# The first modulation weight taken in four channel slices in the front stage of a hybrid decoder layer

## The reference, cut to what matters

```python
mod = jax.nn.silu(c) @ w_ada[l] + b_ada[l]          # 1024 -> 6 x 1024
sh1, sc1, g1, sh2, sc2, g2 = [m[:, None, :] for m in jnp.split(mod, 6, axis=-1)]
u = x * (1.0 + sc1) + sh1
proj = u @ w_in                                     # ... | q | k | v | ...
```

## Time and profile before

| | |
|---|---|
| median of 3 runs | 2750.84 us (2745.45 to 2751.7) |
| profiled execution, its own time | 2748.32 us |
| span of its profile | 2746.4 us |
| PE busy | 2492.0 us, 91% |
| DVE busy | 1461.8 us, 53% |
| ACT busy | 1116.5 us, 41% |
| POOL busy | 831.0 us, 30% |
| DMA | 549.61 MB, mean 200 GB/s |

### The profile page before, as it was taken

The page is one execution under the profiler, slowest core; times in us unless marked ns, Lnnn a source line. Parts: engine busy times, 40 slices in busy tenths (PEclk is TensorE's granted clock), DMA queues, the critical chain, the costliest instruction groups (busy, mean ns, idle before and its releaser), DMA issues. The chain is left out here.

```text
span 2746.4 us, 36119 instructions
## 1 busy us (share of the span) xinstructions
PE 2492.0 (91%) x12521; PEld 2082.2 (76%) x12522; DVE 1461.8 (53%) x1898; ACT 1116.5 (41%) x1818; POOL 831.0 (30%) x707
## 2 busy tenths in 40 slices
PE   5999899999999999999989979995998999999960
PEld 4788678778888888888868858874887888887850
DVE  6222156665665656566653256774447445526636
ACT  3122144554454545454531022213547545526633
POOL 2111022442222222222212226575222222223236
PEclk9999899999999999999999989996999999999985
DMA  7699676767665666676446746433558646627736
GB/s 262 248 311 321 240 219 187 250 199 231 194 214 176 213 210 198 193 244 196 150 157 207 208 154 238 161 108 136 162 153 290 181 142 203 192 61 227 253 70 245
DMA packets 258781, 549.61 MB, mean 200 GB/s; under 512 B 23860, under 2 KB 93608, under 8 KB 258024
## 3 DMA queue, kind: packets, MB, share of 16 engines
q1 hardware_dynamic: 236072, 483.07, 53.0%
q0 software_dynamic: 15248, 46.62, 7.6%
q10 hardware_dynamic: 7344, 18.35, 1.7%
HBM read 394.94 MB, written 153.02 MB: 200 GB/s over the span
## 5 line engine op out<-in xcount | busy, mean ns | idle before, releaser
L93 PE MATMUL mx_acc<-u_u,mx_w_hi 128*128 128x512 f32 x1792 | 569.8, 399 | 4.0 <-DMA mx_w_lo<-halves 4.0
L722 POOL TENSOR_TENSOR mx_wt<-mx_wt,mx_rest 128x127 f32<-128x127 f32 (+15 forms) x128 | 271.5, 2121 | 743.4 <-DVE mx_rest L924 743.4
L93 PEld LDWEIGHTS mx_acc<-u_u,mx_w_hi 128*128 128x128 f32 x1792 | 325.5, 189 | 68.4 <-DMA mx_w_lo<-halves 4.8
L932 DVE TENSOR_TENSOR mx_wt_lo<-mx_p_t,mx_wt_hi 128x512 fp32r<-128x512 f32 (+2 forms) x320 | 192.2, 605 | 326.9 <-ACT mx_wt_hi L887 325.1
L93 PE MATMUL mx_acc<-u_u,mx_w_lo 128*128 128x512 f32 x896 | 352.0, 393 | 0.0
L887 ACT ACTIVATE mx_wt_hi<-mx_p_t 128x512 fp32r<-128x512 f32 (+2 forms) x320 | 170.9, 534 | 408.6 <-PE mx_p_t L774 361.5
L924 DVE TENSOR_TENSOR_SCAN mx_rest<-mx_rest,mx_zero 128x128 f32<-128x128 f32 (+15 forms) x128 | 314.2, 2455 | 8.8 <-ACT mx_wt L869 8.8
L93 PE MATMUL moe_p_gu<-keep_wide_hi,moe_x_hi 128*128 128x512 f32 x656 | 262.6, 400 | 14.1 <-DVE keep_wide_lo L1936 13.0
L93 PE MATMUL moe_p_gu<-keep_wide_hi,moe_x_lo 128*128 128x512 f32 x656 | 258.1, 393 | 0.0
L93 PE MATMUL moe_p_gu<-keep_wide_lo,moe_x_hi 128*128 128x512 f32 x656 | 257.8, 393 | 0.0
L868 ACT ACTIVATE mx_rest<-mx_p_z 128x512 f32<-128x512 f32 (+2 forms) x320 | 171.1, 535 | 100.1 <-PE mx_p_z L761 59.2
(11 more groups left out here) (250 smaller groups left out, 5134.1 us busy)
## 6 DMA issues: line engine op xcount, KB each, us to landing
mx_w_hi<-halves SPq DMA_DIRECT2D x98, 512.0 KB, 3.7
mx_w_lo<-halves SPq DMA_DIRECT2D x98, 512.0 KB, 5.3
keep_stay<-in_w_gate SPq DMA_DIRECT2D x64, 512.0 KB, 5.2
keep_stay<-in_w_up SPq DMA_DIRECT2D x64, 512.0 KB, 6.1
keep_stay<-in_w_down SPq DMA_DIRECT2D x32, 1024.0 KB, 6.9
u_saved<-u_u SPq DMA_DIRECT2D x4, 4096.0 KB, 19.5
mx_w_mod<-in_w_ada SPq DMA_DIRECT2D x64, 256.0 KB, 5.1
gate_t<-mx_g_out SPq DMA_DIRECT2D x64, 256.0 KB, 5.0
```

The costliest lines, as they stand in the source:

```text
L93: mm = pe.matmul(out, a, b, start=first and n == 0, stop=last and n == len(pairs) - 1, skip_group_check=True)
L722: pool.tensor_tensor(wt[:, t % 2, 0:w - 1], wt[:, t % 2, 0:w - 1], rest[:, t % 2, 1:w], ALU.mult).then_inc(m["weights_done"], 1)
L932: dve.tensor_tensor(wt_lo[:, first:first + k - j], p_t[:, n % TR, 0:(k - j) * P].rearrange("p (j t) -> p j t", t=P), f32(wt_hi[:, first:fi ...
```

## The change

The first 2048 columns of `w_ada` are loaded and summed in four slices of 256 shift and 256 scale channels, that is two groups `k` each. A slice is eight DMAs of 256 KB in pieces of 1 KB, into `ada`, a double buffer in `stay`, which nothing else uses in this stage. Slices 1 to 3 are put in SP's queue ahead of weight pieces 2, 4 and 6; slice i waits for the sums of slice i - 2. DVE sums slice i + 1, and adds it to `mod` after PE's column sums, ahead of the weight rests of the two groups of slice i; each of its eight steps waits for the one before. PE's column sums of slices 2 and 3 stand behind parts 1 and 3, in a bank of their own, so that TR is 3. A transpose for part k + 3 now stands behind part k.

For block 0 ACT makes the high part of u itself. The rests of the second column half go from DVE to GpSimd, behind u's eighth rest. ACT takes second-half pieces 8 to 11 ahead of the evictions, 12 and 13 behind that of unit 1, and 14 and 15 behind that of unit 3. SP's weight loads 12 to 15 wait for GpSimd's rests 1 to 4, and `load_x(1)` and `save(0)` still come behind them.

```diff
-    AB, TR = 4, 4
+    AB, TR = 4, 3
...
+        ada = flat(stay, 1).rearrange("p (b k h n) -> p b k h n", b=2, k=KD, h=2)
...
             # gpsimd
+                if n == KD - 1:
+                    for j in range(KD):
+                        pool.wait_ge(m["w_hi_done"], KD + j + 1)
+                        pool.tensor_tensor(w_lo[:, j, WH:2 * WH], ring[:, j % RS, 0:WH], f32(w_hi[:, j, WH:2 * WH]), ALU.subtract
+                                           ).then_inc(m["w2_lo_done"], 1)
...
             # sync
+            def load_slice(i):
+                past(sp, m["summed"], KD * (i - 1))
+                for q in range(SLICES):
+                    for h in range(2):
+                        sp.dma_start(ada[:, i % 2, SK * q:SK * (q + 1), h], ada_view[:, SK * q:SK * (q + 1), h * D + i * SC:h * D + (i + 1) * SC]
+                                     ).then_inc(ada_in[i % 2][q], 16)
+
+            def load_w(n):
+                half, k = divmod(n, KD)
+                if n < KD + RS:
+                    past(sp, m["w_lo_done"], n - RS + 1)
+                else:
+                    sp.wait_ge(m["w2_lo_done"], n - RS - KD + 1)
...
+            load_slice(0)
             sp.dma_start(xr[:], x_view[:, 0]).then_inc(m["x_in"], 16)
             for n in range(2 * KD):
+                if n < KD and n > 0 and n % SK == 0:
+                    load_slice(n // SK)
+                load_w(n)
...
             # tensor
+            sum_rows(0)
             for k in range(TR):
                 turn(0, k)
+            sum_rows(1)
             pe.wait_ge(m["cols_out"], 2)
             for k in range(KD):
+                pe.wait_ge(m["u_lo_done"], k + 1)
+                pe.wait_ge(m["w_lo_done"], k + 1)
+                for i in range(AB):
+                    part(0, i, k)
                 if TR + k < KD:
                     turn(0, TR + k)
+                if (k + 1) % SK == 0 and k // SK + 2 < SLICES:
+                    sum_rows(k // SK + 2)
             for tb in range(TB):
                 for i in range(AB if tb == 0 else 0, UNITS):
                     if tb == 0 and i == WH // P:
-                        pe.wait_ge(m["w_lo_done"], 2 * KD)
+                        pe.wait_ge(m["w2_lo_done"], KD)
...
             # scalar
             for k in range(KD):
+                act.wait_ge(m["mod_step"], k // SK + 2)
                 affine(0, k)
+                act.wait_ge(m["affine"], k + 1)
+                act.activation(u[:, 0, 0, k], uf[:, k % 2], ACT.Copy).then_inc(m["u_hi_done"], 1)
                 high_w(k)
-            for n in range(KD, 2 * KD):
+            for n in range(KD, KD + RS):
                 high_w(n)
...
+                if n in (1, 3):
+                    for j in range(2):
+                        high_w(KD + RS + n - 1 + j)
...
             # vector
+            def sum_slice(i):
+                for k in range(KD):
+                    dve.wait_ge(ada_in[i % 2][k // SK], 32 * (i // 2 + 1))
+                    if k == 0:
+                        ins = dve.tensor_scalar(msum[:, i], ada[:, i % 2, 0], csilu[:, 0:1], None, ALU.mult)
+                    else:
+                        dve.wait_ge(m["summed"], KD * i + k)
+                        ins = dve.scalar_tensor_tensor(out=msum[:, i], in0=ada[:, i % 2, k], scalar=csilu[:, k:k + 1],
+                                                       in1=msum[:, i], op0=ALU.mult, op1=ALU.add)
+                    ins.then_inc(m["summed"], 1)
+                dve.wait_ge(m["mod_summed"], i + 1)
+                dve.wait_ge(m["mod_step"], i + 1)
+                cols, sums = (v.rearrange("p (h k) -> p h k", h=2)[:, :, SK * i:SK * (i + 1)]
+                              for v in (mod[:, 0:FIRST_COLS], p_mod[:, 0:FIRST_COLS]))
+                dve.tensor_tensor(cols, cols, sums, ALU.add).then_inc(m["mod_step"], 1)
...
-            for k in range(KD):
-                high(0, k)
-                low_w(k)
-            for n in range(KD, 2 * KD):
-                low_w(n)
+            sum_slice(0)
+            for i in range(SLICES):
+                if i + 1 < SLICES:
+                    sum_slice(i + 1)
+                for k in range(SK * i, SK * (i + 1)):
+                    low_w(k)
```

More of the change, by code:

```diff
@@ L137, in load_piece, with front @@
             bass.ds(e, 1), :, a - KD:b - KD].rearrange("e p k d -> p (e k) d")).then_inc(piece_in[i], 16)
-def front(nc, used, keep, x, c, w_ada, b_ada, w_conv, w_in, u, u_in, u_saved, qk_hi, qk_lo, v_tok, halves):
+def front(nc, used, keep, stay, x, c, w_ada, b_ada, w_conv, w_in, u, u_in, u_saved, qk_hi, qk_lo, v_tok, halves):
     ident, mod, conv_cols, csilu, one = (keep[n] for n in ("ident", "mod", "conv_cols", "csilu", "one"))
     VR = NJ + KD + 3 * KC
-    MW = FIRST_MOD * NB
     QW, QKW = 3 * AW, 2 * AW
@@ L148, in front @@
     UNITS = QKT + NB // P
-    AB, TR = 4, 4
+    AB, TR = 4, 3
     RS = 4
-    MH, WH = MW // 2, QW // 2
+    WH = QW // 2
+    SLICES = 4
+    SC = D // SLICES
+    SK = KD // SLICES
     c_q = 3 * CH
@@ L155, in front @@
         vec = s.sb("vec", [VR, P])
-        ring = s.sb("ring", [P, RS, MH])
+        ring = s.sb("ring", [P, RS, D])
+        ada = flat(stay, 1).rearrange("p (b k h n) -> p b k h n", b=2, k=KD, h=2)
         xr = s.sb("x", [P, NB // P, D])
@@ L160, in front @@
         stage = s.sb("stage", [P, 2, 2 * NB])
-        acc, p_t = s.ps("acc", [P, AB, NB]), s.ps("p_t", [P, TR, NB])
-        p_vec, p_mod = acc[:, AB - 1, 0:VR], acc[:, AB - 2, 0:FIRST_COLS]
+        acc, p_t, p_mod = s.ps("acc", [P, AB, NB]), s.ps("p_t", [P, TR, NB]), s.ps("p_mod", [P, NB])
+        p_vec = acc[:, AB - 1, 0:VR]
         names = ("vec_in", "vec_turned", "ident_step", "silu_done", "cols_out", "summed", "mod_summed", "mod_step",
-                 "x_in", "turned", "affine", "u_hi_done", "u_lo_done", "w_hi_done", "w_lo_done", "pe_done", "act_out",
+                 "x_in", "turned", "affine", "u_hi_done", "u_lo_done", "w_hi_done", "w_lo_done", "w2_lo_done", "pe_done", "act_out",
                  "dve_out", "fill_hi_done", "fill_lo_done")
@@ L169, in front @@
         ring_in = [s.sem(f"ring_in{i}") for i in range(RS)]
+        ada_in = [[s.sem(f"ada_in{b}{i}") for i in range(SLICES)] for b in range(2)]
         block = ctx.enter_context(nc.Block())
-        msum = stage
+        msum = stage[:].rearrange("p a b -> p (a b)").rearrange("p (s h n) -> p s h n", s=SLICES, h=2)
         x_view = x.rearrange("b (g t p) d -> (b p) g t d", p=P, t=NB // P)
@@ L193, in _ @@
             sp.dma_start(vec[NJ + KD:VR, :], w_conv.rearrange("l t (r p) -> (l t r) p", p=P)).then_inc(m["vec_in"], 16)
[L194 to L198, removed]
+            def load_slice(i):
[10 more added lines that the diff above has]
+                    sp.wait_ge(m["w2_lo_done"], n - RS - KD + 1)
+                sp.dma_start(ring[:, n % RS, 0:WH], in_view[:, k, c_q + half * WH:c_q + (half + 1) * WH]
+                             ).then_inc(ring_in[n % RS], 16)
+            load_slice(0)
             sp.dma_start(xr[:], x_view[:, 0]).then_inc(m["x_in"], 16)
             for n in range(2 * KD):
[L201 to L207, removed]
+                if n < KD and n > 0 and n % SK == 0:
+                    load_slice(n // SK)
+                load_w(n)
             def load_x(tb):
@@ L219, in load_fill @@
                 if n == 0:
-                    sp.wait_ge(m["w_lo_done"], 2 * KD)
+                    sp.wait_ge(m["w2_lo_done"], KD)
                 col = fill_column(n)
@@ L294, in part, with sum_rows @@
                     mm.then_inc(m["pe_done"], 1)
[L296 to L302, removed]
+            def sum_rows(i):
+                pe.wait_ge(m["summed"], KD * (i + 1))
+                for h in range(2):
+                    for j in range(SK):
+                        n = h * KD + i * SK + j
+                        mm = pe.matmul(p_mod[:, n:n + 1], msum[:, i, h, j * P:(j + 1) * P], one[:], start=True, stop=True,
+                                       skip_group_check=True)
+                mm.then_inc(m["mod_summed"], 1)
+            sum_rows(0)
             for k in range(TR):
                 turn(0, k)
+            sum_rows(1)
             pe.wait_ge(m["cols_out"], 2)
             for k in range(KD):
+                pe.wait_ge(m["u_lo_done"], k + 1)
+                pe.wait_ge(m["w_lo_done"], k + 1)
+                for i in range(AB):
+                    part(0, i, k)
                 if TR + k < KD:
                     turn(0, TR + k)
[L309 to L314, removed]
+                if (k + 1) % SK == 0 and k // SK + 2 < SLICES:
+                    sum_rows(k // SK + 2)
             for tb in range(TB):
@@ L341, in high_w @@
                 half, k = divmod(n, KD)
-                act.wait_ge(ring_in[n % RS], 16 * (2 * KD // RS + n // RS + 1))
+                act.wait_ge(ring_in[n % RS], 16 * (n // RS + 1))
                 act.activation(w_hi[:, k, half * WH:(half + 1) * WH], ring[:, n % RS, 0:WH], ACT.Copy
```

(25 more changed lines are left out.)

## The result

The changed kernel takes 2764.26 us (median of 5 runs, 2761.72 to 2764.58); the kernel before took 2747.42 in 5 runs (2742.13 to 2751.7). The ratio is 1.0056, 95% interval 1.0044 to 1.0068: slower, by 16.8 us between the medians. Forecast were 2765.7 and + 14.9.

The account below looks back on a forecast made before the run. Unit 6's start on PE was taken to bound `front`, set by SP's issue of `load_x(1)` and `save(0)`. 7.5 for the queue, 4.9 for the chain and 2.5 for the clock gave + 14.9 us, 2765.7; range 2754 to 2773.

Parts of the forecast that it names:

- The place: Start of unit 6 on PE in `front`: its lateness is handed on one for one; 12.4 us later forecast.
- the chain behind the eviction: From unit 2's eviction to unit 6: ACT's high parts 14 and 15, then two GpSimd rests; 4.9 us more.
- the clock: PE at unit 6: after standing 19 us it runs at the lower clock, 2.5 us more.
- the first term: SP's queue: `load_x(1)` goes out behind GpSimd's four rests, at 69.6 against 62.03, so unit 2's eviction is 7.5 us later.
- The early start: Start of `front`: with slices PE begins part 0 at 29.6 against 41.69, 12.1 us earlier.
- The port: DVE and GpSimd exclude each other at SBUF: each u rest falling into a slice costs DVE 1.3 us.
- What the loop gives back: PE's loop: clock, port and order use up almost all of the 12.1 us; it ends at 66.4 against 65.24.
- The light case: Rival: eviction of unit 2 hardly moves, only the chain behind the stores and the clock stay; + 5.3 us, chance 0.23.
- T: Start of ACT's eviction of unit 2, forecast at 91.4 us against 83.9.
- The other side: Rival: stores are not held up, the early start is kept; up to 12.1 us won, 2739, chance 0.04.

Follow-up runs that it names:

- e1: Changed kernel with ACT's high parts 12 to 15 all behind the eviction of unit 1; 2760.45 us, 1.0051 of the kernel before.
- e6: Changed kernel with 34 more matmuls, result unused, on PE between units 5 and 6; 2758.45 us, 1.0035 of the kernel before.
- e9: Changed kernel with 46 more matmuls, result unused, on PE between units 5 and 6; 2761.93 us, 1.0036 of the kernel before.
- e5: Changed kernel with second-half rests on DVE again and all 16 of ACT's high parts ahead of the evictions, slices kept; 2751.34 us, 1.0014 of the kernel before.
- e8: The kernel of e3 with each slice summed behind the weight rests of the slice before; 2742.66 us, 0.9982 of the kernel before.
- e11: The kernel of e10 with the slices and ACT's high parts of u added; 2739.91 us, 0.9964 of the kernel before.
- e10: Kernel before, load_x(1) ahead of weight load 12, save(0) behind unit 3's stores, high parts and DVE rests 12 to 15 behind unit 1's eviction; 2737.81 us, 0.9955.
- e2: Changed kernel with save(0) queued behind the stores of unit 3; 2751.41 us, 1.0011 of the kernel before.
- e3: Changed kernel with load_x(1) ahead of weight load 12, save(0) behind unit 3's stores, high parts 12 to 15 behind unit 1's eviction; 2742.19 us, 0.9979.
- e4: Kernel before with save(0) moved behind the stores of unit 3; 2743.38 us, 0.9984 of the kernel before.

## Why the prediction was right, step by step

**The place.** Right: what counts is when unit 6 starts, and everything behind it only shifts. Unit 6 came at 99.89 (forecast 97.7), and the mixer 17.5 us later where the sum was 14.9. The medians moved by 16.8.

**The terms.** Measured, with the forecast in brackets: `load_x(1)` 8.5 later (7.5); from it to the eviction of unit 2 1.2 longer, 23.1 against 21.9 (0; e1, e6 and e9, the same kernel up to there, have 22.0, 23.9 and 22.4, so 1.2 is within what equal kernels differ by); the chain behind the eviction 4.84 longer (4.9), shown by e1; the clock 2.9 (2.5), shown by e9. Their sum is the 17.5 at the mixer.

**The reason for the first term.** Its size was right, its reason in part wrong. The working says that for the save the loop's end does not matter, and counts GpSimd's four rests, 7.6 us, as new ahead of `load_x(1)`. Four rests stood there before as well, on DVE, and e5 has `load_x(1)` 6.9 us late without GpSimd: what moves it most is the late end of the sliced loop, handed on through the eighth rest and weight load 11, and the slower engine adds 1.6. The number came out because the working let GpSimd begin only at 61.6, which is the loop's lateness (measured 62.40; u's last rest ended at 57.8 before).

**The early start.** 10.6 us (12.1). DVE began slice 1 at 20.12 and not 19.5, waiting for its DMA: the 1 KB pieces moved 292 GB/s at a share of 0.93 from 4 to 10 us, so 314 at a full one where 350 had been taken. And the slice sums were mis-sized: seven of them without GpSimd take 5.89 us (e8's profile), a step of 0.86 us each with 0.75 of work, where 0.79 had been taken, so a slice is 6.5 and not 6.0. Slice 1 took 7.9 with its meetings (7.3). Below are the durations in the changed kernel:

```profile
L416 DVE SCALAR_TENSOR_TENSOR fr_stage<-keep_stay,keep_csilu,fr_stage x28: 750/752/1587, 6.3 to 51.2; 128x512 f32<-128x512 f32 x28
L413 DVE TENSOR_SCALAR fr_stage<-keep_stay,keep_csilu x4: 486/1280/1508, 5.7 to 43.2; 128x512 f32<-128x512 f32 x4
L195 POOL TENSOR_TENSOR fr_w_lo<-fr_ring,fr_w_hi x8: 1796/1834/2353, 62.4 to 98.0; 128x768 fp32r<-128x768 f32 x8
```

**The port.** DVE's sums, 0.75 us each, and its first step, 0.49, take up to 1.59 and 1.51 where GpSimd works. In e8 they never meet, and all 28 sums take 750 to 754 ns. What one meeting costs is less than the forecast 1.3: the seven sums of slice 1 took 6.70 with one, so 0.8, and the first step of slices 2 and 3 was 1.0 longer; the single durations of 2 us did not come. The trace of before could have shown it for SCALAR_TENSOR_TENSOR: in the mixer L984 takes 0.74 at 384.51, and 1.53 at 440.62, where a GpSimd operation of 3.36 us runs from 438.25. This agrees with the Trainium skill, SBUF — State Buffer, section "Who interferes with whom": a DVE instruction with two SBUF inputs contends with a GpSimd instruction that reads SBUF.

**What the loop gives back.** Right in kind. Part 0 ran at the lower level (first pair 1.19 us at 31.11), and the mean clock of the loop was 0.79. PE ended it at 67.51, 2.3 us after the 65.24 of before (forecast 66.4), so more than the whole early start was given back; unit 4 began 1.0 earlier only because the evictions did. e11 against e10 shows the net of it: slices and ACT's high parts together lose about 3 us even when nothing behind them is held up.

**One stall too few.** The forecast had PE stand 19 us before unit 6. It stood twice, 8.27 us at 82.34 and 8.16 at 99.89: the transposes of block 1 behind unit 4 need x, whose load had gone out at 70.54. The working overlooked that `load_x(1)` is wanted by PE itself. That this cost nothing is luck, since GpSimd's rests set unit 6 anyway; in e2 x and the rests come due together, and PE, late with unit 5 by its wait of 6.69 us for x, starts unit 6 without a wait.

**The rivals.** The light case, + 5.3, was out because T moved by 9.7 us; with the rests on DVE (e5) it still moved by 6.2. The other side, an early start kept, shows in e3 with the queue changed, 4 us and not 12, and e10 shows that even this is not the slices' doing.

## What to carry to other kernels

An engine relieved early wins nothing if its work's results go out through a queue that something late holds up: follow the store that frees the buffer, and ask what stands ahead of it. Moving a 4 MB save that nobody waits for behind the first stores was worth 3 to 4 us at the mixer here; with the next input's load ahead of weights that are needed later, and the high parts and rests of those weights behind the first evictions, it was 8.1 us (337.14 to 329.07), and 0.45% of the time. Slicing the first wait, with ACT's high parts, took about 3 us of it: its start was 10 us earlier, and its loop ended later. When a step moves to a slower engine, count who waits for it, in this case SP's whole queue.

## What was not expected of the hardware

- After a stand of PE of 4.07 us the matmuls stayed long for 5.3 us; after one of 3.73 us for 2.7 (e4); and in e6, after 3.13 us, the first pair took 0.74 and the long ones came only then. A unit with its transposes takes 5.9 us at full clock, and took 8.6, 7.3 and 7.6 there. So the cost of such a stand is not one number. In the changed kernel the matmuls also grew long at 44.03 (pairs of 1.03 to 1.05 up to 46.56), 1.45 us after a wait of only 1.21.
- Two SCALAR_TENSOR_TENSOR steps that depend on each other are 0.86 us apart with 0.75 of duration, and small tensor operations before showed 0.04 for the same: the gap between dependent steps is 0.1 for these.
- A 4 MB save did not visibly slow the load just ahead of it in the queue, only the stores behind it: x's 2 MB took 9.6 to 11.8 us to land in the eight profiles with the save right behind, and 10.1 and 10.2 in e2 and e4 without it; the 256 KB stores behind the save took 19.8 and 21.1 us in the changed kernel.
